# High and low activations side by side: one 512- and one 256-column product per triple in the feed-forward layers and the last down projection

## The reference

```python
def sqrelu_mlp(hn, w1, w2):                      # D_FF = 4096, both layers of the first model
    return jnp.square(jax.nn.relu(hn @ w1)) @ w2
...
x = x + mix
x = x + sqrelu_mlp(rms_norm(x, norm_mlp[i]), mlp_w1[i], mlp_w2[i])
...
# second model, D_FF_2 = 3072
up = causal_dwconv(jnp.einsum("bsd,df->bsf", h, w_up[layer]), conv_f_w[layer], conv_f_b[layer])
gate, val = jnp.split(up, 2, axis=-1)
ffn_out = jnp.einsum("bsf,fd->bsd", jax.nn.gelu(gate) * val, w_down[layer])
x = x + rms_norm_2(ffn_out, ffn_norm_post[layer])
```

## Time and profile before

| what | value |
|---|---|
| runs | 1143.08, 1150.58, 1153.22 us; median 1150.58 us |
| span of the profiled execution | 1135.6 us |
| median less span | 15.0 us |
| PE busy | 1112.7 us, 98% of the span, 9407 products |
| DVE / ACT / POOL busy | 783.6 / 588.2 / 130.6 us |
| granted TensorE clock | 0.997 of full speed on the mean |
| DMA | 192.65 MB, 170 GB/s on the mean |

### The profile page before, as it was taken

How to read it: one execution, slowest core, us unless ns; L and a number is a source line. 1 busy time by engine, 2 the same in 40 slices (tenths; PEclk the granted TensorE clock), 3 DMA queues, 4 the chain that set the end, 5 groups by cost and what they waited for, 6 DMA issues and landing times.

```text
span 1135.6 us, 21644 instructions
## 1 busy us (share of the span) xinstructions
PE 1112.7 (98%) x9407; PEld 1072.3 (94%) x9407; DVE 783.6 (69%) x1127; ACT 588.2 (52%) x829; POOL 130.6 (12%) x87
## 2 busy tenths in 40 slices
PE   7999899999999999999999999999999989999998
PEld 6988799999999899999999999999988979999998
DVE  6567479784457566877743879877465869888752
ACT  4477555443336555544434475654265547666631
POOL 4200040001230004000122301500000000101000
PEclk9999999999999999999999999999999999999999
DMA  9943055566554444556665372556434545666551
GB/s 277 275 152 112 1 186 186 186 198 200 196 186 155 155 137 149 187 185 197 200 197 186 104 227 75 186 187 188 137 129 144 185 134 170 200 201 206 187 185 38
DMA packets 194866, 192.65 MB, mean 170 GB/s; under 512 B 9691, under 2 KB 192964, under 8 KB 194772
## 3 DMA queue, kind: packets, MB, share of 16 engines
q1 hardware_dynamic: 193680, 190.53, 52.4%
q10 hardware_dynamic: 1092, 0.75, 0.4%
HBM read 189.78 MB, written 1.47 MB: 168 GB/s over the span
## 4 chain that ended last, share of the span: by engine, by line
PE 92%; DVE 3%; ACT 2%; DMA 1%; issue 1%; ACTq 0%; SPq 0%; DVEq 0%
PE ps_gemm L1694 48%; PE ps_trans L1694 33%; PE ps_score L1764 2%; PE ps_out L1802 2%; PE ps_trans L1787 2%; PE ps_score L2006 1%; PE ps_out L2006 1%; DVE h_rnn L1463 1%; DMA raw<-in_ev_w_in 1%; DVE w_lo L1118 1%; DVE act_lo L1124 1%; ACT w_hi L736 1%; PE ps_gemm L1874 1%; DMA par_rows<-in_conv_f_w 1%; PE ps_score L1770 0%
## 5 line engine op out<-in xcount | busy, mean ns | idle before, releaser
L1118 DVE TENSOR_TENSOR w_lo<-raw,w_hi 128x2048 fp32r<-128x2048 f32 (+2 forms) x179 | 408.9, 2293 | 45.9 <-ACT w_hi L736 45.8
L736 ACT ACTIVATE w_hi<-raw 128x2048 fp32r<-128x2048 f32 (+2 forms) x179 | 332.6, 1864 | 175.8 <-DMA raw<-in_mlp_w 92.6
L1694 PE MATMUL ps_gemm<-act_hi,w_hi 128*128 128x256 f32 (+1 forms) x960 | 265.9, 285 | 5.7 <-ACT act_hi L1044 4.4
L1694 PE MATMUL ps_gemm<-act_hi,w_lo 128*128 128x256 f32 (+1 forms) x960 | 257.1, 279 | 0.0
L1694 PE MATMUL ps_gemm<-act_lo,w_hi 128*128 128x256 f32 (+1 forms) x960 | 254.1, 280 | 1.3 <-DVE act_lo L1124 1.3
L1694 PEld LDWEIGHTS ps_gemm<-act_hi,w_hi 128*128 128x128 f32 (+1 forms) x960 | 180.5, 190 | 11.0 <-issue 7.6
L1694 PE MATMUL ps_trans<-act_hi,w_hi 128*128 128x256 f32 x688 | 190.5, 277 | 0.0
L1694 PE MATMUL ps_trans<-act_lo,w_hi 128*128 128x256 f32 x688 | 190.3, 277 | 0.0
L1694 PE MATMUL ps_trans<-act_hi,w_lo 128*128 128x256 f32 x688 | 190.3, 277 | 0.0
L1694 PEld LDWEIGHTS ps_gemm<-act_hi,w_lo 128*128 128x128 f32 (+1 forms) x960 | 177.5, 188 | 0.3
L1694 PEld LDWEIGHTS ps_gemm<-act_lo,w_hi 128*128 128x128 f32 (+1 forms) x960 | 173.8, 186 | 3.9 <-DVE act_lo L1124 1.7
(11 more groups left out here) (371 smaller groups left out, 2245.3 us busy)
## 6 DMA issues: line engine op xcount, KB each, us to landing
raw<-in_mlp_w SPq DMA_DIRECT2D x64, 1024.0 KB, 5.4
raw<-in_w_in SPq DMA_DIRECT2D x30, 1024.0 KB, 5.3
raw<-in_w_up SPq DMA_DIRECT2D x24, 1024.0 KB, 5.2
raw<-in_od_w_in SPq DMA_DIRECT2D x12, 1024.0 KB, 5.0
raw<-in_w_down SPq DMA_DIRECT2D x12, 1024.0 KB, 5.2
raw<-in_ev_w_in SPq DMA_DIRECT2D x9, 1024.0 KB, 8.4
raw<-in_w_proj_a SPq DMA_DIRECT2D x8, 640.0 KB, 4.2
raw<-in_ev_w_out SPq DMA_DIRECT2D x4, 1024.0 KB, 5.2
```

Source lines behind the costliest of these rows:

```text
L736: act.activation(w_hi[:, slot, 0:k, 0:n], raw[:, slot, 0:k, 0:n], ACT.Copy).then_inc(hi_done, 1)
L1118: dve.tensor_tensor(w_lo[:, slot, 0:k, 0:n], raw[:, slot, 0:k, 0:n], w_hi[:, slot, 0:k, 0:n].bitcast(F32), ALU.subtract).then_inc(w_ready, 1)
L1694: ins = pe.matmul(dst, lhs, rhs, start=(first and opens and opening), stop=(last and closes and i + 1 == len(order)), skip_group_check=True)
```

## The change

Each pair of a high and a low part now lies in one tensor: `act`, `mix`, `hid`, `ya`, `m2`, `h2` are `[P, 2, ...]`, and so is `w_parts`, the weights; `raw` shares its place with the low weights as before. In the stages `a_up`, `m_up`, the first three groups of `a_dn` and `m_dn`, and the first three of `f_dn` (`WIDE` in the code), a triple is two products: one of 512 moving columns, `w_hi` with `[x_hi, x_lo]` (in `f_dn`: `x_hi` with `[w_hi, w_lo]`), and one of 256, `w_lo` with `x_hi` (in `f_dn`: `x_lo` with `w_hi`). The first slab of each up stage keeps its three products. The fourth groups and all other stages keep triples of 256.

A wide group holds two banks: half h of the result lies in bank h of a pair, columns 0 to 255 (`main`), and the correction from the low activations beside it, columns 256 to 511 (`cor`). ACT copies `cor` to SBUF (one instruction of 128x512), DVE adds it to `main`, which frees the pair. In the up stages `ps_out` is a third pair. The square `up_q` goes from DVE to ACT, and DVE's `split_lo` moves from the head of the step to behind the two steps that follow `slab_done`.

```diff
+    w_parts = place("w_parts", [P, 2, RING, KS, NS], F32R)
+    w_hi, w_lo = w_parts[:, 0], w_parts[:, 1]
...
+    WIDE = {}
+    for name in ("a_up", "m_up"):
+        WIDE.update({st[name].g0 + j: (0, 2, 4) for j in range(16)})
+    for name in ("a_dn", "m_dn"):
+        WIDE.update({st[name].g0 + j: (0, 2, 4) for j in range(3)})
+    WIDE.update({st["f_dn"].g0 + j: (0, 2) for j in range(3)})
...
         # ACT, mlp_up
             for j in range(16):
+                g = g0 + j
+                act.wait_ge(slab_done, s0 + j + 1)
+                act.activation(cor_up[:, j % 2, :, :], cor(g), ACT.Copy).then_inc(cor_ok, 1)
                 split_hi(s0 + j + AHEAD)
-                g = g0 + j
-                act.wait_ge(emptied[BANK[g]], out_count(g))
+                act.wait_ge(upr, l * 16 + j + 1)
                 act.activation(hid_hi[:, 2 * j:2 * j + 2, :], up_r[:, j % 2, :, :], ACT.Square).then_inc(hid_h, 1)
+                if j >= 2:
+                    act.wait_ge(hid_l, l * 16 + j - 1)
+                act.activation(up_q[:, j % 2, :, :], up_r[:, j % 2, :, :], ACT.Square).then_inc(upq, 1)
...
         # DVE, mlp_up
             for j in range(16):
-                split_lo(s0 + j + AHEAD - 1)
                 g = g0 + j
                 dve.wait_ge(slab_done, s0 + j + 1)
-                dve.scalar_tensor_tensor(out=up_r[:, j % 2, :, :], in0=pair(g), scalar=0.0, in1=k_pair, op0=ALU.max,
-                                         op1=ALU.mult).then_inc(emptied[BANK[g]], 1)
+                dve.wait_ge(cor_ok, l * 19 + j + 1)
+                if j >= 2:
+                    dve.wait_ge(upq, l * 16 + j - 1)
+                dve.tensor_tensor(up_r[:, j % 2, :, :], main(g), cor_up[:, j % 2, :, :], ALU.add).then_inc(emptied[BANK[g]], 1)
                 dve.wait_ge(emptied[BANK[g]], out_count(g))
-                dve.tensor_tensor(up_q[:, j % 2, :, :], up_r[:, j % 2, :, :], up_r[:, j % 2, :, :], ALU.mult)\
-                    .then_inc(upr, 1)
-                dve.wait_ge(upr, l * 16 + j + 1)
+                dve.scalar_tensor_tensor(out=up_r[:, j % 2, :, :], in0=up_r[:, j % 2, :, :], scalar=0.0, in1=k_pair,
+                                         op0=ALU.max, op1=ALU.mult).then_inc(upr, 1)
+                split_lo(s0 + j + AHEAD - 1)
+                dve.wait_ge(upq, l * 16 + j + 1)
                 dve.wait_ge(hid_h, l * 16 + j + 1)
...
         # DVE, mlp_dn, for the groups q < 3
+                        dve.wait_ge(cor_ok, l * 19 + 17 + q)
+                        dve.tensor_tensor(x[:, c, :], main(g), x[:, c, :], ALU.add).then_inc(x_main, 1)
+                        dve.wait_ge(x_main, l * 3 + q + 1)
+                        dve.tensor_tensor(x[:, c, :], cor_dn[:, :, :], x[:, c, :], ALU.add).then_inc(emptied[BANK[g]], 1)
...
         # ACT, f_dn, after slabs 2, 5 and 8
+                act.activation(cor_out[:, :, :], cor(st["f_dn"].g0 + gi), ACT.Copy).then_inc(cor_ok, 1)
+                act.wait_ge(emptied[BANK[st["f_dn"].g0 + gi]], out_count(st["f_dn"].g0 + gi))
...
         # PE, gemm
-            passes = ((w_hi, x_hi), (w_hi, x_lo), (w_lo, x_hi))
+            HH, HL, LH, TWO = range(4)
+            each = (HH, HL, LH) if g not in WIDE else (TWO, HL) if tok_major else (TWO, LH)
+            order = [(k, half, q) for k in ks for half in halves for q in each]
...
+                if g in WIDE:
+                    c0 = T if (q == HL and low_last or q == LH and tok_major) else 0
+                    dst = wide(g)[:, half, c0:c0 + (2 * T if q == TWO else T)]
                 if tok_major:
-                    lhs = xx[:, kc0 + k, half * P:(half + 1) * P]
-                    rhs = w[:, slot, k, 0:n]
+                    lhs = x_parts[:, xp, kc0 + k, half * P:(half + 1) * P]
+                    rhs = w_parts[:, :, slot, k, 0:n] if q == TWO else w_parts[:, wp, slot, k, 0:n]
                 else:
-                    lhs = w[:, slot, k, half * P:half * P + mm]
-                    rhs = xx[:, kc0 + k, :]
+                    lhs = w_parts[:, wp, slot, k, half * P:half * P + (m or P)]
+                    rhs = x_parts[:, :, kc0 + k, :] if q == TWO else x_parts[:, xp, kc0 + k, :]
```

More of the change, by code:

```diff
@@ L207, in build @@
     sq_g = ar("sq_gain", [P, 3, 2, T], 64 * K)
[L209 to L213, removed]
+    cor_up = ar("cor_up", [P, 2, 2, T], 64 * K)
+    cor_out = ar("cor_out", [P, TB, NS], 66 * K)
+    hid = ar("hid", [P, 2, NH1, T], 0, F32R)
+    hid_hi, hid_lo = hid[:, 0], hid[:, 1]
+    mix = ar("mix", [P, 2, NX, T], 0, F32R)
+    mix_hi, mix_lo = mix[:, 0], mix[:, 1]
     cw1 = ar("cmp_w1", [P, 2, 16, P], 16 * K)
@@ L358, in build, with banks, holder @@
     BANK = bank_table()
+    def banks(g):
+        return (BANK[g], BANK[g] + 1) if g in WIDE else (BANK[g],)
+    def holder(b, g):
+        return max((i for i in range(g) if b in banks(i)), default=None)
     def out_count(g):
@@ L913, in _ @@
         out_stage("a_out", 1)
-        mlp_up("a_up", 1)
-        mlp_dn("a_dn", 2)
+        mlp_up("a_up", 1, 0)
+        mlp_dn("a_dn", 2, 0)
         root(2)
@@ L936, in _ @@
         act.wait_ge(gain_ok, 1)
[L937 removed]
+        mlp_dn("m_dn", 4, 1)
         root(4)
@@ L1647, in _, with bank_free, gemm @@
     def _(pe):
-        def gemm(s, g, x_hi, x_lo, kc0=0, n_k=KS, first=True, last=True, tok_major=False, n=NS, m=None,
+        def bank_free(g):
+            for b in banks(g):
+                h = holder(b, g)
+                if h is not None:
+                    pe.wait_ge(emptied[BANK[h]], out_count(h))
+                elif b < 2:
+                    pe.wait_ge(emptied[b], 2)
+        def gemm(s, g, x_parts, kc0=0, n_k=KS, first=True, last=True, tok_major=False, n=NS, m=None,
                  before_pair=None, before_chunk=None, low_last=False, between=None, ks=None, opens=True, closes=True,
                  rounds=None, second=None, by_half=None):
-            slot, b, bank = SLABS[s][0], BANK[g], result(g)
+            slot = SLABS[s][0]
             ks = range(n_k) if ks is None else ks
@@ L1673, in gemm @@
             if by_half is not None:
-                order = [(k, half, q) for half in halves for k in ks for q in range(3)]
-            low = [i for i, (_, _, q) in enumerate(order) if q == 2][0]
+                order = [(k, half, q) for half in halves for k in ks for q in each]
+            low = [i for i, (_, _, q) in enumerate(order) if q in (LH, TWO)][0]
+            opened = set()
             for i, (k, half, q) in enumerate(order):
@@ L1697, in gemm @@
                     ins.then_inc(by_half, 1)
-                if between is not None and half == len(halves) - 1 and q == 2:
+                if between is not None and half == len(halves) - 1 and q == each[-1]:
                     between(k)
@@ L1778, in transposes @@
                     for bk in (2, 3):
-                        held = [g for g in range(st[out_name].g0) if BANK[g] == bk]
-                        if held:
-                            pe.wait_ge(emptied[bk], out_count(held[-1]))
+                        h = holder(bk, st[out_name].g0)
+                        if h is not None:
+                            pe.wait_ge(emptied[BANK[h]], out_count(h))
                 if i:
@@ L1945, in out_stage @@
                 early = OUT_EARLY[p][j] if p is not None and j < 2 else []
-                gemm(s, g, h, l, ks=[k for k in range(KS) if k not in early], opens=not early,
+                gemm(s, g, parts, ks=[k for k in range(KS) if k not in early], opens=not early,
                      before_chunk=chunk_ready(p) if p is not None and j < 2 else None,
@@ L1960, in ready @@
                     pe.wait_ge(hid_l, l * 16 + r * 4 + pair + 1)
-                gemm(s0 + j, g0 + j // 4, hid_hi, hid_lo, kc0=(j % 4) * 8, first=j % 4 == 0, last=j % 4 == 3,
+                gemm(s0 + j, g0 + j // 4, hid, kc0=(j % 4) * 8, first=j % 4 == 0, last=j % 4 == 3,
                      before_pair=ready if j < 4 else None)
-        out_stage("a_out", mix_hi, mix_lo, p=0)
+        out_stage("a_out", mix, p=0)
         mlp("a_up", "a_dn", 1, 0)
```

162 lines of the change are left out of this document (94 added, 68 removed).

## The result

| | before | after |
|---|---|---|
| median of the runs | 1150.43 us (1143.08 to 1153.22, 7 runs) | 1158.14 us (1155.25 to 1162.76, 7 runs) |
| ratio, 95% interval | | 1.011 (1.0076 to 1.0144) |
| profiled execution: span | 1135.6 us | 1153.7 us |

What follows compares the result with a forecast made beforehand. The prediction took the pace of products on PE as the bound: 7.6 us saved there, less 1.4 us for the heads, gives 6.2 us less, the median going from 1150.6 to 1144.4 us. Range: 1136 to 1153.5 us.

Steps and rivals of the forecast that it cites:

- the middle reading: Wide stages: a 512-column product has a fixed extra of 6.7 ns and takes 220.0 ns; chance 0.50.
- High end: Upper bound for the 512-column product: the extra grows with the columns, 226.7 ns, a triple 340.0 ns, nothing saved.
- Rival 4: Wide stages: changing lengths puts the stream on the slow level, triple 353.4 ns, 1164.2 us; chance 0.06.
- The level holds from one pause of the stream to the next: PE's stream: a short product's pace, 113.3 or 117.8 ns, stays the same between two pauses.
- triple in wide slabs: All wide stages: one long and one short product, 220.0 + 113.3 = 333.3 ns, 6.7 less than before.
- PE in the up stages, 480 triples: `a_up` and `m_up`: 30 wide slabs of 16 triples, 6.7 ns less each, 3.2 us saved.
- PE in the down stages, 384: `a_dn` and `m_dn`: 24 wide slabs, 2.6 us saved.
- `f_dn`, 144: `f_dn`: nine wide slabs, three at the quick level saving 0.3 us, six at the slow one saving 1.5 us.
- heads of `a_up` and `m_up`: Up stages' starts: PE waits 0.7 us ahead of slab 2 for DVE's split, 1.4 us for two heads.
- 1 (215.8 ns): Rival, wide stages: the long product is as cheap as the plain fp32 one, 1140.3 us; chance 0.18.
- 2 (226.7): Rival, wide stages: the extra grows with the columns, nothing saved on PE, heads cost 1.4 us, 1152.0 us; chance 0.14.
- 3: Rival, stages elsewhere: slow levels change, up to 9 us less, about 1137 us with the saving; chance 0.12.

Runs made afterwards that it cites:

- the benches: Separate kernels computing nothing of the reference: segments of products by themselves, to read the distance between starts; 512 columns alone with 128 stationary columns: 226.7 ns.
- layout_only: The kernel before with only the weight parts' places of the changed kernel, high parts first, low parts and raw behind: 1149.10 us, ratio 1.0004.
- kinds_apart: The changed kernel with each wide slab's 16 long products first, then its 16 short ones: 1150.72 us, ratio 1.0065.
- short_products: The changed kernel with its banks, copies, adds and orders, but three 256-column products per triple again: 1148.51 us, ratio 1.0008.
- down_only: The changed kernel with wide products only in the down stages and `f_dn`, the up stages as in the kernel before: 1152.76 us, ratio 1.0069.
- load_bench: Products by themselves, not the kernel: 256 and 512 columns, alone and in turns, with 16 to 128 stationary columns; pair in turns with 128 and 128: 346.7 ns.

## Why the prediction was wrong

**The step that failed** is "I take the middle reading, a fixed extra per product: 213.3 + 6.7 = 220.0 ns". The extra of a long product is 13.3 ns or more alone in the benches, 18 to 20 ns in the kernel where the lengths are kept apart (230.9 and 232.8), and 22 in turns (235). I took the short product's extra as fixed because the plain fp32 row, 216 ns, said that an extra needn't double. That row is of another type of product and says nothing of float32r at 512 columns: in the kernel the extra goes from 6.7 ns at 256 columns to 18 or more at 512. In the benches with 128 stationary columns it is 13.3 ns at 256, 320, 384 and 512 columns alike. There it is fixed, as I assumed, but at two steps of 6.7; what fails is the one step, which I took over from the kernel's short product.

**The range failed at its high end,** and for the same reason. "High end: the extra grows with the columns, 226.7 ns" was the value of a long product by itself. In the kernel a pair in turns costs 353.3 ns and one apart 346.7, and no row of before could show a pair. Rival 4 had this price, and got 6 chances in 100. The argument against it, "both levels appear within one stage and don't depend on the mix of operands", was about products of one length; it said nothing on changing lengths. An earlier sentence, "The level holds from one pause of the stream to the next", is not so in the trace of before itself: at 777.5 us, with no pause, the distance goes from 118 to 113 ns, where the moving operand changes from weights to activations. In `layout_only` it goes from 113 to 118 ns at the same product (785.9 us). Half of the loss was there with the lengths apart, in the long product alone, above the bound that I took for it.

| term | predicted | measured |
|---|---|---|
| triple in wide slabs | 333.3 ns | 353.3 ns |
| PE in the up stages, 480 triples | -3.2 us | +6.4 us |
| PE in the down stages, 384 | -2.6 us | +5.1 us |
| `f_dn`, 144 | -1.8 us | +0.6 us (six slabs stood at 353.4) |
| heads of `a_up` and `m_up` | +1.4 us | +1.3 us |
| start of `m_dn` | 0 | +1.0 us |
| narrow products behind the wide ones | 0 | +1.9 us |
| clock dip before `a_up` | 0 | +1.6 us |
| rest | 0 | +0.2 us |

The sum of the last column is 18.1 us, the difference of the spans; the last term is what is left of it.

**Rivals.** 1 (215.8 ns) and 2 (226.7) have the long product too cheap. 3 is half true: the levels do move from one execution to the next, but a payback from them was not seen. 4 was right to the digit in the triple (353.4 forecast, 353.3 measured), and that is partly luck. Its mechanism is there: turns of two lengths put the stream on the slow level, which shows in the narrow groups behind them (117.8 ns in six of six, 113.3 in four of four with the lengths apart). But it makes only half of the loss in a triple, and the other half is there without turns (`kinds_apart`, 346.7). Its 1164.2 us was 6 us too high. It was counted from the profiled span and carried over to the median of runs that took longer; in runs like that of `layout_only`, half of these triples already cost 353 ns. An estimate from the traces at hand: with narrow products, the up stages stood at the quick level in five of eight cases (`before` two, `layout_only`, `short_products` and `down_only` one each). 5/8 of 12.1 + 1.9 us is 8.8, with the waits (2.3) 11 us, between the 7.7 us of the medians and the 12.7 us of the ratio on record. Eight cases are few, so this is argued, not shown. Put plainly: a wide triple costs at all times what a narrow one costs on its slow level.

**What held.** That only the pace of products counts. That neither DVE nor ACT becomes the bound and the added work costs nothing measurable (ratio 1.0008 in `short_products`). That a split comes late at the heads alone and not in every step: in the middle of `a_up` the split for the slab that PE starts at 207.9 (two slabs of 5.65 after 196.6) is done at 206.57, 1.3 us early:

```profile
202.26 0.60 ACT L935 ACTIVATE cor_up<-ps_out 128x512 f32<-128x512 f32 x1 [2.21 <-PE ps_out L1767]
...
202.95 0.69 DVE L1380 TENSOR_TENSOR up_r<-ps_out,cor_up 128x512 f32<-128x512 f32 x1 [1.43 <-PE ps_out L1767]
...
204.29 2.28 DVE L1163 TENSOR_TENSOR w_parts<-raw,w_parts 128x2048 fp32r<-128x2048 f32 x1
```

The copy took 0.60 us (0.59 worked out), the add 0.69. The heads were forecast nearly right, 1.3 us for 1.4: the slower slab ahead takes part of the wait away, and the restart of the stream adds 0.1 us to each. The bank pairs never made PE wait.

**What was not looked at** is the hand-over from `m_up` to `m_dn`, with a table load and a chain of small instructions on DVE. Its 1.0 us is hidden in the spread, but the step "in the down stages ... both engines idle half of this stretch" overlooked it.

**The pages.** The Trainium skill (TensorE: Matmul & The Clock Gate, section "Back-to-back issue gap") spoke against the change, and came nearer than I did, but its sign too was wrong: it leaves a gain of 2.5 ns a triple, where 13.3 were lost. By its formula a long product takes 215.8 ns; the measured 226.7 to 235 ns is well above that. That it fits the plain fp32 row, as the prediction says, holds only if such a product counts as 512 columns; for its 256 the formula gives 109.2 ns, and the row has 216. Its other statement in that section, that spacing in a stream is set by the load and the product together, agrees with `load_bench` for 256 columns (113.3 ns with 16 stationary columns, 120.0 with 128) and does not explain the 512-column rows.

## What to carry to other kernels

Fewer, longer products need not be cheaper for being fewer: when PE is the bound, measure the pair of lengths as it will be issued, in the order in which it will be issued, before anything is built on it. The price of a product that no row shows is not bounded by rows of other types, and not by the product alone when it will stand among others. A bench helps only if it also reproduces the price of what is replaced: here the bench's pair (353.3 ns) against the kernel's own triple (340.0) would have warned, while inside the bench (353.3 against 360.0) the change looks like a gain. Where the profiled execution is shorter than every timed run, a change counted against its span needn't carry over to the median.

## What the runs showed of the hardware

- Many settled distances lie on a grid of 6.67 ns, 16 cycles at 2.4 GHz: 113.3, 120.0, 226.7, 340.0, 346.7 and 353.3 ns are 17, 18, 34, 51, 52 and 53 steps. The slow level of the kernel, 353.4 for three products, is 53 steps for what the quick one does in 51, and the bench's 360.0 is 54. Others lie between the steps (115.9, 131.7, 202.7, 231.6, 344.6 ns). A pair of a long and a short product in turns takes 53 steps in every wide stage of the three kernels profiled with it.
- The level of a stream of short products can change without a pause, where the operands change roles: 118 to 113 ns at 777.5 us in the trace of before, 113 to 118 at the same product in `layout_only`. Turns of 512 and 256 columns leave the narrow group behind them on the slow level (six of six), 16 and 16 or four and four leave it on the quick one (four of four). What picks the level of short products alone is open.
- In the benches a float32r product of 256 columns costs the same with 64 stationary columns as with 16, and more with 128: 113.3 against 120.0 ns. My prediction said that the load has no part, from a slab with 16 stationary columns at 113.5 ns; in the kernel 128 columns reach 113.3 as well, in some stages and executions, and why they do there and never did in the bench is open.
- A moving operand of two runs costs the same as one of one run: 226.7 ns for 512 columns, 173.3 for 384, 120.0 for 256, either way.
